# Rebuilding the front of a hybrid MLA and pooling block: scale first, shift as an output row, angles on GpSimd

## The chip, the cores and the metric

The kernel runs on one core of a Trainium2 chip. The metric is the device time of one execution in microseconds (us). Engines are named as the profile names them: PE is TensorE, DVE is VectorE, ACT is ScalarE, POOL is GpSimd, SP is the engine that issues nearly all transfers. "PEld" is PE's weight load.

## The reference, cut to what matters

One encoder block over 1024 tokens of width 1024, in float32. The change touches what comes before attention:

```python
c_act = jax.nn.silu(c)
mod = c_act @ w_ada + b_ada                      # w_ada: 1024 x 6144
sh1, sc1, gt1, sh2, sc2, gt2 = jnp.split(mod, 6)
h = rmsnorm(x, g_mix) * (1.0 + sc1) + sh1
proj = h @ w_in                                  # 960 columns
# proj[..., :448]: q latent 256, kv latent 128, key rope 64; proj[..., 448:]: 4 pool groups of 128
c_q, c_kv = rmsnorm(cq_raw, g_q), rmsnorm(ckv_raw, g_kv)
cos, sin = cos(positions * freqs), sin(positions * freqs)
```

Then come the queries, chunk-causal attention in latent space, the pooling mixer (trailing sums over 2, 4, 8 and 16 tokens, minus u), the output projection gated by gt1, and a SwiGLU network with a last norm.

## The kernel before

Every engine runs a list of instructions written out by hand, in order; semaphores are the only ties between the lists. A float32 matrix product runs as three products of rounded parts (`PASSES`, L46): each operand has a high part (written by `..._hi` functions on POOL or ACT) and a low part, full minus high (the `..._lo` functions and the helper `lo` on DVE, which all show as L1313). x is kept as 8 token tiles of 128; `HT` holds the normed, modulated x transposed, by 8 feature tiles k.

**Modulation.** `w_ada` comes in pieces of 1 MB (`ada_piece`, `load_ada`, L411). DVE sums eight of them, by `accumulate` (L1301, four instructions of 128x512 a piece), to sc1 and gt1 before attention. The 1024 columns of sh1 are done on PE instead (L1868), copied to a row (L892) and turned. The eight sh1 and sc1 pieces come first on SP, then x, then `w_in`.

**Front.** DVE also computes the rope angles (L1322 to L1328, 20 instructions of 128x256 that reduce them by parts of 2 pi), the inverse roots (`inverse_root`, L1266 to L1277, a chain of 12 small instructions) and x times its root (`xn1`, L1309). PE turns a tile of x (`turn_x1`, L1884), ACT scales and shifts it into `HTf` (`modulate1`, L875), POOL takes the high part (`HT`, L673), DVE the low part (`h_lo`). For each token tile PE then runs 24 products against the first 448 columns of w_in (`WTM`, L1900). ACT copies the result to `TMO` and sums its squares (`tm_out`, L883 to L885).

**Between front and attention.** `pool_group(i)` (48 products of 128x512, in the helper `product`, L1841) gives u of a group transposed; `u_out` copies it. `WU` has two slots, so `load_wu(2)` waits for `u_done` 2. DVE norms the latents (`tm_norm`), POOL rotates the keys (L688 to L697, `kr_ready`), rounds `CKV`, `WP` and `WUV` and then runs `windows`: for each of four groups 4, 3, 2 and 1 additions of 128x1024 (L714), two small instructions, and a wait for `pooled(i)` on DVE (L1420). `turn_latents` (L1919) turns `TMO`, with `lt_hi` on ACT and `lt_lo` on DVE behind it. Behind the windows on POOL are eight rotations of the queries (`rotate`, L731 to L735), without which PE's loop of `q_nope`, `q_latent` and `turn_rope` can't run. Attention scores begin at L2015.

## Time and profile before

| | us |
|---|---|
| median of 3 runs | 1037.54 (1037.45 to 1038.49) |
| the profiled execution's own time | 1039.98 |
| its span | 1038.2 |

| engine | busy us | share of span |
|---|---|---|
| PE | 992.2 | 96% |
| PEld | 815.9 | 79% |
| DVE | 676.5 | 65% |
| ACT | 447.7 | 43% |
| POOL | 410.0 | 39% |

The span is the time from the first to the last recorded instruction. Times in rows are from the span's start. A busy PE is a share of time only; PEclk is the clock granted to it, 1.00 being 2.4 GHz and 0.50 being 1.2 GHz. Where PE is busy throughout, what other engines do beside it costs nothing, so the stretches that matter to a change in the front are those in which PE isn't full: the first 46 us and the time from 114 to 182 us.

### The profile page before, as it was taken

Reading aid. Unit: us, or ns where it says so; the run is one execution under the profiler, and the core shown is the slowest. Engines: PE = TensorE matmul, PEld = TensorE weight load, DVE = VectorE, ACT = ScalarE, POOL = GpSimd, SP = SyncE. Lnnn points to the kernel's source line nnn. Section 1 sums busy time; section 2 is a strip of 40 time slices with the busy share of each in tenths; the row PEclk is TensorE's granted clock in tenths of the full one; section 3 lists DMA queues with packets and bytes.
Section 4 is the critical chain, followed back from the end, with each engine's and each line's share of the span. In section 5 each row is a group of like instructions: output and inputs, shape, how many; then the busy total and the mean of one; then the engine's idle time right before and its main releaser. Section 6 shows DMA issues by size and latency. Waiting matters only on the chain.

```text
span 1038.2 us, 12646 instructions
## 1 busy us (share of the span) xinstructions
PE 992.2 (96%) x4605; PEld 815.9 (79%) x4605; DVE 676.5 (65%) x957; ACT 447.7 (43%) x759; POOL 410.0 (39%) x306
## 2 busy tenths in 40 slices
PE   5799989999999999989999999999999999999995
PEld 0598877788888887868888888888888888888884
DVE  5848865767524589956746745844846864747867
ACT  0663246867621466532333333333234442634442
POOL 1313666499603121054643643644642300037510
PEclk9699999999899999989999999999999999999998
DMA  9902110544113333356356255255357998755513
GB/s 325 362 1 102 42 41 1 175 131 127 55 53 111 102 122 101 113 177 207 112 170 205 102 180 186 104 180 182 125 159 261 340 353 312 253 200 172 196 71 153
DMA packets 119929, 165.20 MB, mean 159 GB/s; under 512 B 8694, under 2 KB 61754, under 8 KB 119868
## 3 DMA queue, kind: packets, MB, share of 16 engines
q1 hardware_dynamic: 119868, 164.40, 47.1%
q8 instruction: 37, 0.61, 0.2%
q14 instruction: 24, 0.20, 0.1%
HBM read 124.26 MB, written 40.11 MB: 158 GB/s over the span
## 4 chain that ended last, share of the span: by engine, by line
PE 78%; DVE 11%; ACT 3%; issue 2%; POOL 2%; DMA 2%; SPq 2%; DVEq 0%; POOLq 0%; ACTq 0%
PE PS L2137 39%; PE PS L2171 16%; PE PS L1841 14%; PE PS L1900 4%; PE PS L2015 3%; DMA ADA<-in_w_ada 1%; PE PS L2027 1%; DVE GT L1301 1%; DVE RS L1277 1%; POOL ropeQ L731 1%; ACT PR L986 1%; DVE RT L1273 1%; PE PS L2087 1%; POOL WIN L714 1%; DVE XD L1815 1%
## 5 line engine op out<-in xcount | busy, mean ns | idle before, releaser
L2171 PE MATMUL PS<-RE 128*128 128x512 f32 x924 | 210.5, 390 | 0.0
L2171 PEld LDWEIGHTS PS<-RE 128*128 128x128 f32 x924 | 173.5, 188 | 36.7 <-ACT DU L1217 0.4
L1313 DVE TENSOR_TENSOR RE<-REraw,RE 128x1024 fp32r<-128x1024 f32 x77 | 107.0, 1426 | 73.8 <-ACT RE L1149 73.0
L2137 PE MATMUL PS<-HT,WS 128*128 128x512 f32 x528 | 125.9, 395 | 4.6 <-ACT U L1132 4.6
L1149 ACT ACTIVATE RE<-REraw 128x1024 fp32r<-128x1024 f32 x77 | 81.4, 1061 | 103.3 <-DMA REraw<-t_scratch 67.9
L2137 PE MATMUL PS<-HB,WS 128*128 128x512 f32 x528 | 123.3, 389 | 0.0
L2137 PEld LDWEIGHTS PS<-HT,WS 128*128 128x128 f32 x528 | 100.9, 191 | 26.2 <-issue 5.0
L2137 PEld LDWEIGHTS PS<-HB,WS 128*128 128x128 f32 x528 | 99.2, 188 | 20.5
L2137 PE MATMUL PS<-HT,W 128*128 128x512 f32 x480 | 110.8, 390 | 0.0
L2137 PEld LDWEIGHTS PS<-HT,W 128*128 128x128 f32 x480 | 90.0, 188 | 18.6
L1691 DVE TENSOR_TENSOR SG<-PS,PV 128x512 f32<-128x512 f32 x22 | 15.1, 684 | 106.7 <-PE PS L2137 106.7
L1103 ACT ACTIVATE WS<-WSf 128x1024 fp32r<-128x1024 f32 x42 | 44.6, 1063 | 65.6 <-POOL WSf L791 42.1
L814 POOL TENSOR_TENSOR TW<-TW 128x512 f32<-128x512 f32 x11 | 23.5, 2138 | 111.4 <-PE PS L2137 94.2
L1313 DVE TENSOR_TENSOR WS<-WSf,WS 128x1024 fp32r<-128x1024 f32 x42 | 51.2, 1222 | 20.8 <-POOL WSf L786 14.5
L2137 PE MATMUL PS<-HB,W 128*128 128x512 f32 x264 | 61.6, 389 | 0.0
L783 POOL TENSOR_TENSOR WSf<-W34raw 128x1024 f32<-128x1024 f32 x9 | 21.5, 2391 | 94.9 <-PE PS L2137 94.9
L2137 PEld LDWEIGHTS PS<-HB,W 128*128 128x128 f32 x264 | 49.6, 188 | 10.3
L1142 ACT ACTIVATE SG<-SG 128x512 f32<-128x512 f32 x33 | 20.9, 632 | 78.0 <-DVE SG L1691 78.0
L1841 PE MATMUL PS<-HT,WU 128*128 128x512 f32 x192 | 44.6, 392 | 0.0
L1900 PE MATMUL PS<-WTM,HT 128*128 128x448 f32 x192 | 42.6, 382 | 1.5 <-DVE HT L1313 1.5
L836 POOL TENSOR_TENSOR DP<-DP,GT 128x512 f32<-128x512 f32 x4 | 5.2, 1299 | 98.0 <-DVE GT L1377 98.0
L1841 PEld LDWEIGHTS PS<-HT,WU 128*128 128x128 f32 x192 | 36.0, 188 | 7.8 <-issue 0.5
(261 smaller groups left out, 1874.2 us busy)
## 6 DMA issues: line engine op xcount, KB each, us to landing
REraw<-h_scratch SPq DMA_DIRECT2D x77, 256.0 KB, 4.9
h_scratch<-SG SPq DMA_DIRECT2D x55, 256.0 KB, 2.4
ADA<-in_w_ada SPq DMA_DIRECT2D x12, 1024.0 KB, 8.2
TW<-in_w_down SPq DMA_DIRECT2D x22, 512.0 KB, 4.4
t_scratch<-TW SPq DMA_DIRECT2D x44, 256.0 KB, 5.0
REraw<-t_scratch SPq DMA_DIRECT2D x44, 256.0 KB, 5.1
REraw<-in_w_down SPq DMA_DIRECT2D x33, 256.0 KB, 6.5
X<-in_x SPq DMA_DIRECT2D x16, 512.0 KB, 9.3
```

The lines of the kernel that those rows point to most:

```text
L783: pool.tensor_tensor(WSf[:, SLOT[5], LO], W34raw[:, :, 0:HK], W34raw[:, :, HK:KT], ALU.add).then_inc(S["w_sum"], 1)
L814: then(pool.tensor_tensor(b22, b22, b12, ALU.subtract))
L1103: act.activation(WS[:, SLOT[p], HI], full, ACT.Copy).then_inc(S["w_hi"], 1)
L1142: act.activation(SG[:, q, :], SG[:, q, :], ACT.Silu).then_inc(S["silu"], 1)
L1149: act.activation(RE[e][:, HI], REraw[e][:, LO], ACT.Copy).then_inc(S["d_hi"], 1)
L1313: dve.tensor_tensor(out_, full, hi.bitcast(F32), ALU.subtract).then_inc(ready, 1)
L1691: dve.tensor_tensor(dst, PS[:, y, :], part[:, m, :], ALU.add).then_inc(S["c_add"], 1)
L1841: ins = pe.matmul(ps, l, r, start=(n_ == 0), stop=(n_ == len(terms) - 1))
L1900: ins = pe.matmul(PS[:, 4 + t % 2, 0:TM], HT[:, a, k, tok(t)], WTM[:, b, k, :], start=(k == 0 and p == 0), stop=(k == KT - 1 and p == 2))
L2015: ins = pe.matmul(bank, l, r, start=(z == 0), stop=(z == 4 and not diag))
L2137: ins = pe.matmul(PS[:, bank, :], l, r, start=fresh and z == 0, stop=z == len(terms) - 1, skip_group_check=not fresh)
L2171: ins = pe.matmul(PS[:, D_BASE[p] + j, :], RE[e][:, a, 0, tok(j)], RE[e][:, b, 1, :], start=p in (1, 2, 7) and i == 0 and x_ == 0, stop=i ...
```

## The change

- **Loads.** SP brings the four sc1 pieces (`load_sc1`) in the place of sh1: two at once, then x 0 to 3, half of `WTM`, the other two sc1 pieces, the rest. The sh1 pieces become the first of DVE's list (`DVE_CHUNKS`), later than `sc1_sum` 2. The gt1 pieces get four places of their own (`GTP`), three of which lie where `WTM` is, so pieces 5 to 7 wait for `bias_row` and the latents' `LT` (at 96 KB) waits for `acc_done` 8 on ACT.
- **Scale.** Pieces 0, 1 and 3 are summed on DVE (`scale_sum`), piece 2 on POOL (`ACCP`); PE turns each half (`scale_turn`) and DVE makes four columns of G1 (`scale_columns`), so that the first four feature tiles can go before the scale of the others is known. PE's work on the first four token tiles is split in feature halves.
- **Shift.** ACT only multiplies by G1, straight into the high part of `HT` (`scaled_hi`), and DVE takes the low part from PSUM (`scaled_lo`); `HTf` and POOL's L673 are gone here. sh1 times the 448 columns is one row from 16 narrow products (`shift_row`), spread to all partitions by `shift_all` and added to `TMO` on DVE in four instructions (`tm_bias`). The squares of the latents (`tm_squares`) wait for that and follow `u_out(0)` on ACT.
- **Angles** move from DVE to POOL, each fused instruction as two, ahead of `wtm_hi(0)`. The scaling of x 4 to 7 moves from DVE to POOL.
- **Order behind.** `wu_hi(2)` is ahead of the key rotation on POOL and `wu_lo(2)` ahead of the norms on DVE; the two norms share one `inverse_root`. `accumulate(6)` and `(7)` come between the norms and `CKV`'s low part. `col_sum(2)`, `(3)` and the `gate` copies move from ahead of the last pool group to just ahead of PE's query loop. 40 transposes of the identity (`keep_clock`) stand ahead of the first `scale_turn`.

```diff
...
-    ADA0 = at("ADA0", 32, [P, 4, 4, HALF])
...
-    SHROW = at("SHROW", 180, [P, 2, HALF])
+    ACCP = at("ACCP", 180, [P, HALF])
+    GTP = [at(f"GTP{i}", kb, [P, 4, HALF]) for i, kb in enumerate((0, 96, 104, 112))]
+    BROW = at("BROW", 182, [P, HALF])
...
-    DVE_CHUNKS = (2, 3, 4, 5, 10, 11)
+    DVE_CHUNKS = (0, 1, 4, 5, 10, 11)
...
+        if 4 <= j < 8:
+            return GTP[j - 4][:], sc1_in[j - 4], 32
+        ring, turn = (ADA1, j // 2) if j < 4 else (ADA3, j // 2 - 2)
+        return ring[:, j % 2], ada_in[j % 2], 16 * (turn + 1)
...
+            if j == 0:
+                sp.wait_ge(S["sc1_sum"], 2)
+            elif j in (2, 3, 10, 11):
...
+        load_sc1(0)
+        sp.dma_start(POSI[:], positions.rearrange("b (t p) -> p (b t)", p=P), allow_slow_non_contiguous=True).then_inc(S["pos_in"], 16)
+        sp.dma_start(FREQ[:], freqs.partition_broadcast(P)).then_inc(S["freq_in"], 16)
+        load_sc1(1)
+        load_x(0)
         for src, r, n in ((b_ada, 0, 48), (g_mix, ROW_MIX, 8), (g_ffn, ROW_FFN, 8), (pool_scale, ROW_POOL, 4)):
             sp.dma_start(ROWS[r:r + n, :], src.rearrange("l (r n) -> (l r) n", n=P)).then_inc(S["rows_in"], 16)
-        sp.dma_start(POSI[:], positions.rearrange("b (t p) -> p (b t)", p=P), allow_slow_non_contiguous=True).then_inc(S["pos_in"], 16)
-        sp.dma_start(FREQ[:], freqs.partition_broadcast(P)).then_inc(S["freq_in"], 16)
-        load_sh1(1)
-        load_ada(1)
-        load_sh1(2)
-        load_ada(2)
-        load_sh1(3)
-        load_x(0)
-        load_ada(3)
-        for t in range(1, 4):
-            load_x(t)
-        for i in range(4):
-            sp.dma_start(WTMraw[:, 2 * i:2 * i + 2, :], win_d[:, 2 * i:2 * i + 2, 0:TM]).then_inc(wtm_in[i], 16)
+        load_x(1)
+        load_x(2)
+        load_x(3)
+        load_wtm(0)
+        load_wtm(1)
+        load_sc1(2)
+        load_sc1(3)
+        load_wtm(2)
+        load_wtm(3)
...
-        sp.wait_ge(S["sh1_rows"], 1)
+        sp.wait_ge(S["sc1_sum"], 1)
         load_wu(0)
         load_wu(1)
+        for j in range(3):
+            load_ada(j)
+        sp.wait_ge(S["t1"], 2 * KT)
+        sp.dma_start(WPraw[:], w_pool.rearrange("l g c d -> c (l g) d")).then_inc(S["wp_in"], 16)
         load_ada(4)
+        load_ada(3)
+        sp.wait_ge(S["acc_done"], 4)
+        sp.dma_start(WUQraw[:], wuq_d).then_inc(S["wuq_in"], 16)
+        sp.dma_start(WUKraw[:], w_uk.rearrange("l c h d -> c (l h) d")).then_inc(S["wuk_in"], 16)
+        sp.wait_ge(S["bias_row"], B["bias_row"] + 1)
+        sp.dma_start(WUVraw[:], w_uv.rearrange("l c h v -> c (l h) v")).then_inc(S["wuv_in"], 16)
         load_ada(5)
-        sp.wait_ge(S["t1"], NT)
-        sp.dma_start(WPraw[:], w_pool.rearrange("l g c d -> c (l g) d")).then_inc(S["wp_in"], 16)
         load_ada(6)
         load_ada(7)
-        sp.wait_ge(S["tm_done"], NT)
-        sp.dma_start(WUVraw[:], w_uv.rearrange("l c h v -> c (l h) v")).then_inc(S["wuv_in"], 16)
         sp.wait_ge(S["u_done"], 2)
         load_wu(2)
         sp.wait_ge(S["u_done"], 4)
         load_wu(3)
-        sp.wait_ge(S["acc_done"], 8)
...
+        pool.wait_ge(S["cast"], B["cast"] + 1)
+        pool.wait_ge(S["freq_in"], 16)
+        for t in range(NT):
+            ins = pool.tensor_scalar(ANG[:, t, :], FREQ[:], POSF[:, t:t + 1], 0.0, ALU.mult, ALU.add)
+        then(ins)
+        for turns in (4096.0, 1.0):
+            then(pool.tensor_scalar(TURN[:], ANG[:], float(1 / (2 * np.pi * turns)), ROUND_MAGIC, ALU.mult, ALU.add))
+            then(pool.tensor_scalar(TURN[:], TURN[:], -ROUND_MAGIC, 0.0, ALU.add, ALU.add))
+            for part in two_pi_parts():
+                then(pool.tensor_scalar(SHALF[:], TURN[:], -part * turns, 0.0, ALU.mult, ALU.add))
+                ins = pool.tensor_tensor(ANG[:], SHALF[:], ANG[:], ALU.add)
+                if (turns, part) != (1.0, two_pi_parts()[-1]):
+                    then(ins)
+        ins.then_inc(S["ang_ready"], 1)
...
+        wtm_hi(0)
+        wtm_hi(1)
+        pool.wait_ge(S["act_silu"], 1)
+        pool.wait_ge(sc1_in[2], 16)
+        then(pool.tensor_scalar(ACCP[:], ADAS[:, 2, 0, :], CS[:, 0:1], 0.0, ALU.mult, ALU.add))
+        for t in range(1, 4):
+            then(pool.tensor_scalar(ADAS[:, 2, t, :], ADAS[:, 2, t, :], CS[:, t:t + 1], 0.0, ALU.mult, ALU.add))
+            ins = pool.tensor_tensor(ACCP[:], ACCP[:], ADAS[:, 2, t, :], ALU.add)
+            if t < 3:
+                then(ins)
+        ins.then_inc(S["sc1_part"], 1)
+        wtm_hi(2)
+        wtm_hi(3)
+        pool.wait_ge(S["rs1"], 2)
+        for t in range(4, NT):
+            pool.tensor_scalar(X[:, t, :], X[:, t, :], RS[:, t:t + 1], 0.0, ALU.mult, ALU.add).then_inc(S["xn1"], 1)
...
+        wu_hi(2)
+        pool.wait_ge(S["tm_bias"], B["tm_bias"] + 4)
         pool.wait_ge(S["trig_ready"], 1)
         pool.memset(U[:, :, 0:PADW], 0.0)
         keys = TMO[:, :, QR + LAT:TM].rearrange("p t (a d) -> p t a d", a=2)
         then(pool.tensor_tensor(both[:, :, :, 1], twice(ropeK[:, 1, :, 0]), twice(ropeK[:, 0, :, 1]), ALU.add))
         pool.memset(WIN[:, :, 0:PADW], 0.0).then_inc(S["kr_ready"], 1)
-        wu_hi(2)
...
+        def scaled_hi(q):
+            hf, k = divmod(q, KT)
+            act.wait_ge(S["t1"], q + 1)
+            act.wait_ge(S["modcols"], 1 if k < 4 else 2)
+            act.activation(HT[:, HI, k, half(hf)], PS[:, k % 4, :], ACT.Copy, scale=G1[:, k:k + 1]).then_inc(S["h_hi"], 1)
...
+            act.activation(TMO[:, t, 0:TM], PS[:, 4 + t % 4, 0:TM], ACT.Copy).then_inc(S["tm_out"], 1)
+        def tm_squares(t):
+            act.wait_ge(S["tm_bias"], B["tm_bias"] + t // 2 + 1)
+            act.activation(JUNK2[:, 0:QR], TMO[:, t, 0:QR], ACT.Square, accum_out=SS[:, t:t + 1])
+            act.activation(JUNK2[:, QR:QR + LAT], TMO[:, t, QR:QR + LAT], ACT.Square,
+                           accum_out=SS[:, 8 + t:9 + t]).then_inc(S["tm_sq"], 1)
+            act.wait_ge(S["tm_sq"], B["tm_sq"] + t + 1)
...
+        for t in range(4):
             squares1(t)
-        for t in range(NT):
-            modulate1(t)
-            if t < 4:
-                squares1(t + 4)
-            if t >= 3:
-                tm_out(t - 3)
-        for t in range(NT - 3, NT):
+        for q in range(4):
+            scaled_hi(q)
+        for t in range(4, NT):
+            squares1(t)
+        for q in range(4, KT):
+            scaled_hi(q)
+        tm_out(0)
+        tm_out(1)
+        for q in range(KT, KT + 4):
+            scaled_hi(q)
+        tm_out(2)
+        tm_out(3)
+        for q in range(KT + 4, 2 * KT):
+            scaled_hi(q)
+        act.wait_ge(S["ang_ready"], 1)
+        act.activation(SHALF[:], ANG[:], ACT.Sin, scale=0.5)
+        act.activation(SQUART[:], ANG[:], ACT.Sin, scale=0.25).then_inc(S["sin_ready"], 1)
+        for t in range(4, NT):
             tm_out(t)
+        act.wait_ge(S["bias_row"], B["bias_row"] + 1)
+        act.activation(BROW[0:2, 0:TM], PS[0:2, 3, 0:TM], ACT.Copy).then_inc(S["bias_out"], 1)
...
         u_out(0)
+        for t in range(NT):
+            tm_squares(t)
         u_out(1)
+        act.wait_ge(S["acc_done"], 8)
         for t in range(4):
             lt_hi(t)
...
+        dve.tensor_copy(POSF[:], POSI[:]).then_inc(S["cast"], 1)
...
+        def scaled_lo(q):
+            hf, k = divmod(q, KT)
+            dve.wait_ge(S["h_hi"], q + 1)
+            dve.scalar_tensor_tensor(HT[:, LO, k, half(hf)], PS[:, k % 4, :], G1[:, k:k + 1],
+                                     HT[:, HI, k, half(hf)].bitcast(F32), ALU.mult, ALU.subtract).then_inc(S["h_ready"], 1)
...
+        scale_sum(ACC[:, 0], 0, 1)
+        dve.wait_ge(S["rowsT"], 1)
+        dve.tensor_copy(COLS[:], PS[:, 6, 0:N_ROWS]).then_inc(S["cols"], 1)
+        dve.wait_ge(S["cols"], 1)
+        scale_columns(0)
+        roots1(0, 4)
+        scaled_lo(0)
+        wtm_lo(0)
+        scaled_lo(1)
+        scaled_lo(2)
+        wtm_lo(1)
+        scaled_lo(3)
+        scale_sum(ACC[:, 1], 3)
+        roots1(4, 4)
+        scale_columns(1)
+        scaled_lo(4)
+        wtm_lo(2)
+        scaled_lo(5)
+        wtm_lo(3)
+        scaled_lo(6)
+        scaled_lo(7)
+        accumulate(0)
+        for q in range(KT, KT + 4):
+            scaled_lo(q)
...
+        for q in range(KT + 4, 2 * KT):
+            scaled_lo(q)
...
+        accumulate(1)
+        accumulate(2)
         wu_lo(1)
+        accumulate(3)
+        dve.wait_ge(S["colsum"], 2)
+        then(dve.tensor_tensor(MOD[:, 0:8], PS[:, 2, 0:8], COLS[:, 0:8], ALU.add))
+        pair = SHP[:].rearrange("p (k a) -> p k a", a=2)
+        then(dve.tensor_copy(pair[:, :, HI], MOD[:, 0:8]))
+        lo(pair[:, :, LO], MOD[:, 0:8], pair[:, :, HI], S["sh1_ready"])
...
+        dve.wait_ge(S["bias_all"], B["bias_all"] + 1)
+        shift = PS[:, 2, 0:TM].rearrange("p (o n) -> p o n", o=1).broadcast_to([P, 2, TM])
+        for i in range(4):
+            dve.tensor_tensor(TMO[:, 2 * i:2 * i + 2, 0:TM], TMO[:, 2 * i:2 * i + 2, 0:TM], shift, ALU.add).then_inc(S["tm_bias"], 1)
+        accumulate(5)
+        wu_lo(2)
+        dve.wait_ge(S["tm_sq"], B["tm_sq"] + NT)
+        dve.tensor_scalar(VAR[:, 0:8], SS[:, 0:8], 1.0 / QR, EPS, ALU.mult, ALU.add)
+        then(dve.tensor_scalar(VAR[:, 8:16], SS[:, 8:16], 1.0 / LAT, EPS, ALU.mult, ALU.add))
+        inverse_root(None, None, 16, None, S["rs1"])
+        dve.wait_ge(S["rs1"], 3)
...
+        accumulate(6)
+        accumulate(7)
...
-        accumulate(6)
...
-        accumulate(7)
...
+        def scale_turn(i):
+            pe.wait_ge(S["sc1_acc"], i + 1)
+            if i == 1:
+                pe.wait_ge(S["sc1_part"], 1)
+            for k in range(4):
+                col = PS[:, 7, 8 + 4 * i + k:9 + 4 * i + k]
+                ins = pe.matmul(col, ACC[:, i, k * P:(k + 1) * P], ONES[:, 0:1], start=True, stop=i == 0)
+                if i == 1:
+                    ins = pe.matmul(col, ACCP[:, k * P:(k + 1) * P], ONES[:, 0:1], start=False, stop=True)
+            ins.then_inc(S["sc1_sum"], 1)
...
+        keep_clock(40)
+        scale_turn(0)
+        turn_x1(0, 0, range(4))
+        project(0, 0, 4)
+        project(1, 0, 4)
+        project(2, 0, 4)
+        scale_turn(1)
+        turn_x1(0, 4, range(4))
+        project(3, 0, 4)
+        project(0, 4, KT)
+        project(1, 4, KT)
+        turn_x1(1, 0, range(4, NT))
+        project(2, 4, KT)
+        project(3, 4, KT)
+        turn_x1(1, 4, range(4, NT))
+        for t in range(4, NT):
+            project(t, 0, KT)
+            if t == 5:
+                col_sum(0)
+            if t == 6:
+                col_sum(1)
...
+                    ins = pe.matmul(PS[0:2, 3, 0:TM], SHP[:, 2 * k:2 * k + 2], WTM[:, a, k, :],
...
+        shift_row()
+        pool_group(0, (0,))
+        shift_all()
+        pool_group(0, (1,))
         pool_group(1)
+        pool_group(2, (0,))
...
+        pool_group(2, (1,))
         for t in range(4, NT):
             turn_latents(t)
-        col_sum(2)
-        col_sum(3)
         pool_group(3)
...
+        pe.wait_ge(S["wuk_ready"], 1)
+        col_sum(2)
+        col_sum(3)
...
```

## Rows read from the trace of the kernel before

**Rows 1.** Chain that ended last, 46 to 183 us: start us, us, what.
```profile
46.40 7.34 PE PS L1900 x24
...
65.22 0.87 PE PS L1884 x8
66.10 4.85 PE PS L1900 x24
...
92.14 21.78 PE PS L1841 x96
...
131.96 1.91 POOL WIN L714
...
153.47 2.42 POOL ropeQ L731 x2
...
182.16 2.32 PE PS L2015 x10
```

**Rows 2.** Windows of stretches: us, busy us (instructions) by engine, PEclk, DMA, GB/s.
```profile
52.00:92.00 40.00, 40.00 (x218) 37.20 (x217) 22.00 (x39) 23.25 (x77) 8.38 (x7) 1.00 0.05 12
```

**Rows 3.** Timeline, first landings: start us, us, engine, line, operation.
```profile
9.53 0.49 DVE L1299 TENSOR_SCALAR ACC<-ADA,CS 128x512 f32<-128x512 f32 x1 [9.53 <-DMA ADA<-in_w_ada]
```

**Rows 4.** Groups of instructions by line and form: busy us, mean ns.
```profile
L1328 DVE SCALAR_TENSOR_TENSOR ANG<-TURN,ANG 128x256 f32<-128x256 f32 x10 | 4.3, 425 | 0.3
...
L1313 DVE TENSOR_TENSOR QN<-PS,QN 128x512 fp32r<-128x512 f32 x8 | 5.5, 692 | 11.2 <-ACT QN L970 11.1
```

**Rows 5.** Groups by line and form, POOL, 0 to 300 us: busy us, mean ns.
```profile
L731 POOL TENSOR_TENSOR ropeQ<-QRAW,COS 128x256 f32<-128x256 f32 x8 | 5.9, 739 | 5.4 <-DVE U L1420 3.3 <-PE PS L1982 1.6
...
L705 POOL TENSOR_SCALAR WP<-WPraw 128x512 fp32r<-128x512 f32 x1 | 0.6, 619 | 0.0
```

**Rows 6.** Timeline of POOL, the first window sums, 118 to 125 us.
```profile
118.12 1.38 POOL L677 TENSOR_SCALAR WU<-WUraw 128x1024 fp32r<-128x1024 f32 x1
119.47 5.11 POOL L714 TENSOR_TENSOR WIN<-WIN 128x1024 f32<-128x1024 f32 x2
```

**Rows 7.** Chain, `accumulate(6)` beside those sums, one step of `accumulate(7)` alone.
```profile
120.07 2.28 DVE GT L1301
...
122.37 2.77 DVE GT L1301
...
128.29 0.76 DVE GT L1301
```

**Rows 8.** Timeline, 95 to 102 us: small DVE instructions beside POOL and alone.
```profile
95.32 1.43 POOL L688 TENSOR_TENSOR ropeK<-TMO,COS 128x256 f32<-128x256 f32 x2
...
96.11 0.65 DVE L1275 TENSOR_TENSOR RT<-RS 128x8 f32<-128x8 f32 x1
...
98.19 0.17 DVE L1275 TENSOR_TENSOR RT<-RS 128x8 f32<-128x8 f32 x1
...
101.44 3.26 DVE L1397 SCALAR_TENSOR_TENSOR TMO<-TMO,RS,GQ 128x256 f32<-128x256 f32 x8
```

**Rows 9.** Timeline of the front: transposes, x's scaling, the squares of a latent.
```profile
36.77 3.67 PE L1884 MATMUL PS<-IDENT,X 128*128 128x128 f32 x16 [2.56 <-DVE X L1309]
...
53.46 1.42 DVE L1309 TENSOR_SCALAR X<-X,RS 128x1024 f32<-128x1024 f32 x2
...
59.11 0.38 ACT L884 ACTIVATE JUNK<-PS 128x256 f32<-128x256 f32 x1
```

**Rows 10.** Timeline, the third pool group's weights: issue, then their rounding.
```profile
103.05 0.37 SPq L447 DMA_DIRECT2D WUraw<-in_w_in  x1
...
106.98 1.07 POOL L677 TENSOR_SCALAR WU<-WUraw 128x1024 fp32r<-128x1024 f32 x1 [6.03 <-DMA WUraw<-in_w_in]
```

**Rows 11.** Timeline, 110 to 132 us: normed latents reach POOL, first window copy, column sum.
```profile
110.11 1.97 POOL L701 TENSOR_SCALAR CKV<-TMO 128x1024 fp32r<-128x1024 f32 x1 [2.06 <-DVE TMO L1402]
...
130.65 1.22 DVE L1420 SCALAR_TENSOR_TENSOR U<-WIN,U 128x1024 f32<-128x1024 f32 x1
130.67 1.13 PE L1853 MATMUL PS<-GT,ONES 128*128 128x512 f32 x2 [1.52 <-DVE GT L1301]
```

239 lines of the change are left out of this document (98 added, 141 removed).

## The prediction

> **What bounds the kernel now.** The page comes first: PE is busy for 96% of the span, so a change in the front can pay only where PE waits or does other work than before. The chain that ended last gives these places [rows 1]. PE's products of the front begin at 46.40 us; from there it runs without a gap, shown for 52 to 92 us in [rows 2]: a tile of x is eight transposes of 0.87 and 24 products of 4.85 together. The pool groups begin at 92.14 (I call this point S). From 114 on the chain leaves PE: window sums on POOL (131.96) and query rotations on POOL (153.47) lead to the first scores at 182.16. Behind that all work is released by other work, so what is won or lost at 182 us is won or lost at the end. Three places are to be priced: the start to S, S to the rotations (61.3 us), the rotations to the scores (28.7 us).
>
> **What POOL and DVE do to each other.** This decides the case. One step of an accumulation takes 0.76 us on DVE alone, and 2.28 and 2.77 beside POOL's window sums [rows 7]; the two sums that fall there take 5.11 where one is 1.9 [rows 1, 6]. 1.9 + 1.9 + 0.76 is 4.6: they take turns, and each waits for the other's whole instruction. Small ones do too: 0.65 instead of 0.17 beside a rotation of 0.74, and one gets through at 98.19, where POOL itself had to wait for a semaphore [rows 8]. I price it so: a DVE instruction that reads SBUF starts when POOL's current one ends (some 0.2 us early) and puts POOL off by 0.55; those that read PSUM keep their 0.69 [rows 4] and are free of it.
>
> **Part 1, start to S.** Removed: the sh1 row on PE, its copy, 20 angle instructions of DVE (0.43 each [rows 4]), POOL's roundings of x.
> - Landings: before, 2.1 MB are there at 9.53 [rows 3]. Now 1 MB of sc1 is ahead of the positions: taken at 7 us; the second piece again at 9.5.
> - Angles on POOL: an addition of 128x256 is 0.74, a 128x512 multiplication 0.62 [rows 5]; for 128x256 I take 0.40 (an estimate between that and half of it). 8 small ones at 0.2, 14 at 0.40, 10 at 0.74 and 24 gaps of 0.08 (the semaphore steps) make 16.5. DVE's eight steps for the scale and four scalings of x put them off by about 7. POOL is through at 31.6 (7.2 + 16.5 + 7, rounded up by the order), `wtm_hi(0)` at 32.6, `wtm_lo(0)` one turn later at 34.4.
> - The other way to the first product: scale summed at 15; 40 transposes in front of `scale_turn(0)`, from 12 us (their list waits for `ROWS`, behind 2.6 MB), 0.23 each at first, as in [rows 9], later half of that, as in [rows 1], to 19; G1 at 21; the roots at 25 (two small steps per POOL instruction); x scaled at 29.4 (0.71 [rows 9] and a turn each); `scaled_lo(0)` at 31.5. So the wait for POOL ends last, and the first product is at 34.5 instead of 46.4.
> - Then DVE and POOL have to do, by turns, the rest of WTM (six of 1.0), POOL's part of the scale (4 of 0.62, 3 of 1.3), piece 3 on DVE (4 of 0.76), roots (2.3), four scalings of x; the low part of the first four features ends at 38.5, the scale's second half is ready at 44.2, G1's at 47.6, `scaled_lo(7)` at 53.3. PE has 36 products of 0.20 and 4 us of small ones and transposes up to there, and waits for some 5 us.
> - From 53.9 PE is full again: 12 + 24 products and the second half's turns 10.8, four tiles of 4.85, two column sums 2.1 (like the one of 1.13 [rows 11]), shift row 16 x 0.19 = 3.1. S is at 89.4, 2.7 earlier. Of 12 us won at the first product 9 are lost again. The sh1 pieces lie in this: `accumulate(3)` ends at 79, `col_sum(1)` needs it at 80; a late piece would cost one for one.
>
> **Part 2, S to the rotations.** PE: half a pool group 5.45, `shift_all` 1.1, the rest to S+12.0 and S+22.9, `pool_group(2)`'s half to S+28.4. Beside it:
> - shift added on DVE, four of 1.1, to S+11; `accumulate(5)` to S+14. Then `wu_lo(2)`: its weights are only asked for after `u_done` 2 (S+12.0), and issue to rounding takes 3.9 and 1.1 [rows 10]: S+17.1. On SP, gt1's pieces 5 to 7 and `WUV` are ahead of those weights, 3.4 MB at S, but at the rate of [rows 3] and better they are in by S+12. Queued behind that wait are the norms on DVE and, on POOL, the key rotation. `tm_squares` ends at S+19.3 (eight times 0.38 and three shorter [rows 9]). 13 steps of the root beside the key rotation end at S+24.7, 16 norm products (3.26 for the first eight [rows 8]) at S+30.2. Before, POOL gets the normed latents at 110.11 [rows 11], S+18.0: 12.2 later. PE waits 1.8 for its first transposes.
> - `accumulate(6)` and `(7)` now stand between the norms and everything of the latents, and ACT waits for `acc_done` 8. They fall beside CKV, WP, WUV, the window sums and `wu_hi(3)` on POOL, eight instructions of 11 us in all, and eight steps of DVE by turns: 11 + 8 x 0.55 is S+45.8. Then CKV's low part, four `lt_lo`, `wu_lo(3)` S+51.3, `pooled(0)` S+52.7; before it started at 130.65 [rows 11], S+38.5. PE has no work from S+38 to S+48.
> - From `pooled(0)` on it is the chain of before (windows 1 to 3, about 22.8 from its start to 153.47), less 1.2 for the gate copies that move away. Rotations at S+74.3 instead of S+61.3: 13.0 later.
>
> **Part 3, rotations to scores.** `col_sum(2)` and `(3)` are now ahead of `q_nope(0)`: 2 x 1.13 [rows 11] in a loop in which PE and POOL await one another; bounds 0 and 2.3, I take 1.9, since q_nope has nothing else in front of it. Their old place is worth nothing: PE waits there for `accumulate(7)` as it is.
>
> **Sum.** -2.7 + 13.0 + 1.9 = +12.2. On the profiled execution's 1039.98 that is 1052.2, on the median of 1037.54, which lies 2.4 lower, 1049.7.
>
> **A rule of the Trainium skill.** For a fused addition of DVE the rows have 0.43 and for POOL's 0.74, a ratio of 1.7 [rows 4, 5]. The Trainium skill (GPSIMD Engine Reference, section 3.1) measures 1.96 for an addition of 2048 elements; by it the ten additions would be 0.9 longer in all (an estimate from that page). By its section 8, GpSimd contends with DVE instructions that have two SBUF inputs or run in a 2-port mode, without a price; the trace agrees, and gives the price.
>
> **Rivals.**
> 1. *Faster: the two engines hinder each other less than I charge.* It decides at two places: whether POOL has the angles done by 24 us instead of 31.6, and whether `accumulate(6)`, `(7)` run at 0.76 a step. Then S is 8 earlier (the first product near 27, PE warm and full sooner), tm_norm is at S+27, lt_lo(0) at S+35, PE's pool groups go through, and the rotations start at S+60: -8 - 1.5 + 1.9 = -7.6, 1030. For it: plain chains of small steps leave gaps, and some of POOL's recorded time is not port time. Against: [rows 6 to 8]. Chance 0.17.
> 2. *Front as in rival 1, middle as forecast*: -8 + 13 + 1.9 = +7, 1044.5. For it: the angle instructions are short. Chance 0.13.
> 3. *Slower still: in the front only one small DVE step gets through per POOL instruction.* The roots then end at 28.5 and x at 33, products begin at 36.5, every turn of the next part is a full instruction, and S is 3.5 later than before; in the middle the same adds 2.4: +3.5 + 15.4 + 1.9 = +20.8, 1058.3. For it: the 0.65 beside back-to-back instructions [rows 8]. Against: these chains wait for semaphores. Chance 0.18.
> 4. *No change*: a shorter stall behind acc_done 8 meets the gain of the front, within 0.2% (2.1 us, what a measurement of this kernel can tell). Chance 0.06.
>
> **Chances and range.** The forecast has 0.46, its own range 1046 to 1055. Slower by over 0.2%: 0.46 + 0.13 + 0.18 = 0.77; same 0.06; faster 0.17. The range goes from 1034, which takes in rivals 2 and 4 and leaves out most of rival 1, to 1059, which takes in rival 3.
>
> **What would show it.** In the profile of the changed kernel: (1) the last angle addition on POOL near 31 us and the first front product near 34.5, released by DVE's low part of WTM; (2) DVE's scale steps above 1 us each; (3) S near 89; (4) the root chain behind `wu_lo(2)`, waiting for POOL's WU; (5) the steps of `accumulate(6)`, `(7)` at 1.5 to 2.7 and ACT's first `LT` copy released by DVE's GT; (6) a hole of some 10 us in PE before the second four transposes of the latents; (7) first rotation near 164, first scores near 194. I am wrong if `accumulate(6)` to `(7)` take 6 us, or if the weights of the third group land so early that the norms don't wait.

## The result and the profile after

The changed kernel takes 1052.13 us (median of four runs, 1049.83 to 1054.30) against 1037.51 (four runs of the kernel before beside them): a ratio of 1.014, 95% interval 1.0124 to 1.0156: slower by 1.4%. Its profiled execution took 1052.04 us with a span of 1050.0; that of before took 1039.98 with 1038.2.

The chain that ended last in the changed kernel (start us, us, what) shows the three stretches of the prediction:

```profile
53.55 3.97 PE PS L1980 x18
...
90.56 5.46 PE PS L1923 x24
...
163.21 2.41 POOL ropeQ L774 x2
...
193.32 2.32 PE PS L2140 x10
```

The first product (shown below) stands at 34.30 instead of 46.40, the pool groups at 90.56 instead of 92.14, the first rotation at 163.21 instead of 153.47, the first scores at 193.32 instead of 182.16 [rows 1]. The front gives back 10.5 of the 12.1 us that it won, and the stretch behind it loses 11.3. From the scores to the end of the span it is 856.7 us against 856.0, so between these two executions nearly all of the difference lies ahead of the scores.

The front, from the timeline of POOL (start us, us, engine, line, operation; in brackets the idle time before it and what ended that):

```profile
8.94 4.18 POOL L684 TENSOR_SCALAR ANG<-FREQ,POSF 128x32 f32<-128x32 f32 x8 [4.85 <-DMA FREQ<-freqs]
...
30.68 0.72 POOL L691 TENSOR_TENSOR ANG<-SHALF,ANG 128x256 f32<-128x256 f32 x1
31.38 1.83 POOL L698 TENSOR_SCALAR WTM<-WTMraw 128x896 fp32r<-128x896 f32 x2
```

of DVE:

```profile
23.80 3.93 DVE L1362 TENSOR_SCALAR X<-X,RS 128x1024 f32<-128x1024 f32 x4
29.07 0.75 DVE L1384 SCALAR_TENSOR_TENSOR HT<-PS,G,HT 128x512 fp32r<-128x512 f32 x1 [1.34 <-ACT HT L914]
32.34 1.81 DVE L1366 TENSOR_TENSOR WTM<-WTMraw,WTM 128x896 fp32r<-128x896 f32 x1 [2.52 <-POOL WTM L698]
```

and of PE:

```profile
34.30 10.38 PE L1980 MATMUL PS<-WTM,HT 128*128 128x448 f32 x36 [5.40 <-DVE WTM L1366]
44.52 0.28 PE L1951 MATMUL PS<-ONES,ACC 128*128 128x1 f32 x2
```

The angles begin at 8.94, when their frequencies have landed, and end at 31.4. WTM's first rounding waits behind them, DVE's half of it (32.34) behind that, and the first product behind that; the feature of x that it needs too had been ready at 29.8. The 36 products that follow take 10.38 us. PE had stood idle for 4.39 and 5.40 us before them, and its granted clock is 0.50 from 25 to 40 us. Up to 40.2 us a product starts every 0.37 us, from there on every 0.21; the mean of all is 0.29. The groups of PE from 35 to 40 us and from 41 to 44 us (busy us, mean ns of one; the records of neighbours overlap):

```profile
L1980 PE MATMUL PS<-WTM,HT 128*128 128x448 f32 x15 | 6.0, 590 | 5.4 <-DVE WTM L1366 5.4
...
L1980 PE MATMUL PS<-WTM,HT 128*128 128x448 f32 x16 | 3.5, 368 | 0.0
```

The middle, DVE:

```profile
97.07 4.08 DVE L1472 TENSOR_TENSOR TMO<-TMO,PS 128x896 f32<-128x896 f32 x4 [9.10 <-PE PS L2021]
...
120.67 12.57 DVE L1354 SCALAR_TENSOR_TENSOR GT<-GTP,CS,GT 128x512 f32<-128x512 f32 x8
133.28 3.25 DVE L1366 TENSOR_TENSOR CKV<-TMO,CKV 128x1024 fp32r<-128x1024 f32 x1
...
141.44 1.21 DVE L1504 SCALAR_TENSOR_TENSOR U<-WIN,U 128x1024 f32<-128x1024 f32 x1
```

and, in the same stretch, ACT's first copy of a turned latent and PE's second group of turns:

```profile
133.28 0.49 ACT L963 ACTIVATE LT<-PS 128x384 fp32r<-128x384 f32 x1 [19.13 <-DVE GT L1354]
```

```profile
137.34 3.01 PE L2038 MATMUL PS<-IDENT,TMO 128*128 128x128 f32 x13 [9.09 <-DVE KRT L1366]
```

The eight steps of `accumulate(6)` and `(7)` take 12.57 us, where alone they would take 6.1 (0.76 each [rows 7]). ACT had waited 19.13 us for them, and PE stands idle for 9.09.

The kernels of the experiments below stand in the same table. Their distances are given from the start of the pool groups, S, so that a front that came out a little sooner doesn't hide in them. "Rotation to scores" is in us:

| kernel | S | norms done | pooled(0) | first rotation | rotation to scores | scores at |
|---|---|---|---|---|---|---|
| before | 92.14 | S+17.9 | S+38.5 | S+61.3 | 28.7 | 182.16 |
| forecast | 89.4 | S+30.2 | S+52.7 | S+74.3 | 30.6 | 194.3 |
| changed | 90.56 | S+30.2 | S+50.9 | S+72.7 | 30.1 | 193.32 |
| angles late | 90.45 | S+30.2 | S+50.9 | S+72.7 | 32.1 | 195.29 |
| sums cut | 88.79 | S+30.3 | S+45.0 | S+66.9 | 30.2 | 185.87 |
| squares first | 88.51 | S+26.0 | S+47.9 | S+69.7 | 31.2 | 189.41 |
| column sums back | 90.59 | S+30.2 | S+50.9 | S+72.6 | 28.7 | 191.92 |
| pieces early | 88.44 | S+30.3 | S+45.0 | S+66.8 | 30.2 | 185.40 |
| middle reordered | 88.79 | S+36.5 | S+36.4 | S+66.4 | 30.2 | 185.40 |
| angles late, idle transposes | 89.5 | S+30.7 | S+51.3 | S+73.1 | 31.4 | 193.98 |
| idle transposes | 88.81 | S+30.2 | S+50.9 | S+72.7 | 30.1 | 191.64 |
| all of these | 88.53 | S+36.5 | S+36.4 | S+68.5 | 28.7 | 185.80 |
| window 0 early | 89.13 | S+37.2 | S+37.1 | S+66.9 | 30.1 | 186.17 |
| the same, angles late | 90.55 | S+37.2 | S+37.1 | S+66.5 | 30.2 | 187.18 |
| window 0 behind roots | 91.27 | S+34.2 | S+34.1 | S+64.4 | 30.2 | 185.80 |

### The profile page after: what moved, and what is told of

Read it like the earlier page. It is cut to its first block, busy times and chain, and to the rows that moved or that the text cites. A ratio compares the mean times of both kernels' runs of the same rounds, so it can differ in the third digit from the quotient of the medians.

```text
span 1050.0 us, 12710 instructions
## 1 busy us (share of the span) xinstructions
PE 987.8 (94%) x4639; PEld 819.7 (78%) x4639; DVE 682.6 (65%) x925; ACT 436.2 (42%) x711; POOL 436.1 (42%) x341
## 4 chain that ended last, share of the span: by engine, by line
PE 77%; DVE 11%; POOL 5%; ACT 3%; issue 2%; DMA 1%; SPq 0%; POOLq 0%; DVEq 0%; ACTq 0%
PE PS L2262 39%; PE PS L2296 16%; PE PS L1923 12%; PE PS L1980 4%; PE PS L2140 3%; POOL WIN L757 1%; DVE GT L1354 1%; DVE RS L1330 1%; PE PS L2152 1%; POOL ANG L691 1%; ACT PR L1038 1%; POOL ropeQ L774 1%; DMA FREQ<-freqs 1%; PE PS L2212 1%; DVE RT L1326 1%
## 5 line engine op out<-in xcount | busy, mean ns | idle before, releaser
L2296 PEld LDWEIGHTS PS<-RE 128*128 128x128 f32 x924 | 173.5, 188 | 36.4 <-issue 0.5
L2262 PEld LDWEIGHTS PS<-HT,W 128*128 128x128 f32 x480 | 90.9, 190 | 18.9
L1980 PEld LDWEIGHTS PS<-WTM,HT 128*128 128x128 f32 x192 | 37.4, 200 | 11.7 <-issue 6.9
```

Source lines behind the costliest of these rows:

```text
L1980: ins = pe.matmul(PS[:, 4 + t % 4, 0:TM], HT[:, a, k, tok(t)], WTM[:, b, k, :], start=(k == 0 and p == 0), stop=(k == KT - 1 and p == 2), ...
L2262: ins = pe.matmul(PS[:, bank, :], l, r, start=fresh and z == 0, stop=z == len(terms) - 1, skip_group_check=not fresh)
L2296: ins = pe.matmul(PS[:, D_BASE[p] + j, :], RE[e][:, a, 0, tok(j)], RE[e][:, b, 1, :], start=p in (1, 2, 7) and i == 0 and x_ == 0, stop=i ...
```

## The experiments

The kernels of each comparison ran between runs of the kernel before on the same chip, whose medians were 1038.27, 1037.12, 1037.27 and 1037.13 us in the order told here (angles late, sums cut, squares first and column sums back; pieces early, middle reordered, idle transposes and all of these; window 0 early and the two others with angles late; the last). All differences of single kernels below some 2 us are read from the traces.

### The angles late

The angle block of POOL is moved as a whole:

```diff
-        pool.wait_ge(S["cast"], B["cast"] + 1)
...
-        ins.then_inc(S["ang_ready"], 1)
         wtm_hi(0)
         wtm_hi(1)
...
         wu_hi(0)
         wu_hi(1)
+        pool.wait_ge(S["cast"], B["cast"] + 1)
...
+        ins.then_inc(S["ang_ready"], 1)
         wu_hi(2)
```

> The changed kernel with one move: the angle instructions on POOL stand behind the rounding of the first two pool groups' weights instead of ahead of the first piece of WTM. Theory (POOL and DVE take turns, and POOL's angle chain sets the first product): without POOL's chain beside it DVE's scale and root steps run at 0.76 and 0.20, the first front product is at about 29 us instead of 34.3, PE is full from 47 instead of 53.6, the pool groups begin near 84 instead of 90.6, and the rest keeps its distances: 6.5 us faster than the changed kernel, about 1045.5. Rival (the tail of the front waits for the sh1 pieces, whose loads and sums come late): the second column sum waits for accumulate(3), the pool groups don't begin before 88, at most 2.5 us faster.

Measured: 1053.83 us (1053.23 to 1055.03), ratio 1.0152 [1.0134, 1.0169], and S at 90.45. Nothing is gained. That lies within the rival's "at most 2.5 us faster", but not for its reason: PE goes from its products into the second column sum (81.17) without a wait, and the pool groups follow as before. The timeline of DVE and PE in the front:

```profile
25.65 5.97 DVE L1362 TENSOR_SCALAR X<-X,RS 128x1024 f32<-128x1024 f32 x4
32.96 0.75 DVE L1384 SCALAR_TENSOR_TENSOR HT<-PS,G,HT 128x512 fp32r<-128x512 f32 x1 [1.34 <-ACT HT L914]
33.62 1.08 DVE L1366 TENSOR_TENSOR WTM<-WTMraw,WTM 128x896 fp32r<-128x896 f32 x1
```

```profile
34.85 10.50 PE L1980 MATMUL PS<-WTM,HT 128*128 128x448 f32 x36 [2.06 <-DVE WTM L1366]
```

POOL is free of the angles, and the first product is no earlier: 34.85. What gets in the way now is POOL's next work. Its share of the scale starts at 21.98, when its piece lands, and runs beside DVE's roots and scalings of x: the scalings start at 25.65 instead of 23.80 and take 5.97 us for the four instead of 3.93, the first feature is begun at 32.96 instead of 29.07, and WTM's low part, which DVE takes behind it, at 33.62. In the changed kernel the short angle steps (0.4 and 0.7) were what stood beside DVE there, and they cost it less than the 1.3 us additions do. What the wait for the angles cost, 4.5 us from the feature to the product, is lost again to the same contention in another place.

### Idle transposes, and both together

The second experiment on the front gives PE something to do in its idle time, so that the clock is up when the products come:

```diff
         keep_clock(40)
         scale_turn(0)
+        keep_clock(28)
         turn_x1(0, 0, range(4))
+        keep_clock(36)
         project(0, 0, 4)
```

> The changed kernel with 28 more idle transposes on PE behind the first column sums of the scale and 36 more behind the first turn of x, in stretches in which PE otherwise waits for DVE. Nothing else differs. In the changed kernel the granted clock is 0.50 from 25 to 40 us, the first 36 products take 10.4 us (0.29 each) and end when the second column sums start, at 44.5. Theory (PE's clock, not the scale's sum, sets the second column sums): granted clock near 1.0 from 25 us on, first product still at 34 to 34.5, the 36 products in 7.8 to 8.2 us, second column sums at 42, pool groups at 88 to 88.5 instead of 90.6, median 1049 to 1050. Rival (the scale's second half, summed on DVE and POOL, is ready at 44 and sets the end): products end at 42, second column sums still at 44 to 44.5, pool groups at 90 to 90.6, median within 0.5 us of the changed kernel's.

Measured: 1049.86 us (1048.01 to 1051.31), ratio 1.0126 [1.0104, 1.0149], S at 88.81. PE:

```profile
34.69 7.58 PE L1980 MATMUL PS<-WTM,HT 128*128 128x448 f32 x36
42.44 0.35 PE L1951 MATMUL PS<-ONES,ACC 128*128 128x1 f32 x2 [0.18 <-POOL ACCP L708]
```

0.21 us a product instead of 0.29 in the mean, as the theory has it, and the second column sums begin at 42.44 instead of 44.52. The wait in front of them, 0.18, is for POOL's share of the scale: the rival's bound is there, but at 42.4 and not at 44. The first product is later than it might be, since my own 36 transposes run until 34.6.

The gain of 1.8 us in S isn't theirs, though. In "middle reordered", whose front is that of the changed kernel without them, S is at 88.79 too:

```profile
33.50 9.87 PE L1980 MATMUL PS<-WTM,HT 128*128 128x448 f32 x36 [3.56 <-DVE WTM L1366]
43.21 0.28 PE L1951 MATMUL PS<-ONES,ACC 128*128 128x1 f32 x2
...
51.74 4.03 PE L1980 MATMUL PS<-WTM,HT 128*128 128x448 f32 x18 [1.05 <-DVE HT L1384]
```

0.8 us won at the column sums are gone again where PE gets full, 51.81 against 51.74, since there PE waits for DVE's features in both. What S goes with is the end of the first eight angle steps. They end between 11.5 and 12.4 us in all seven kernels with the angles in their place that have S at 88.4 to 89.1, and at 13.1 and 13.2 in the changed kernel and in "column sums back", with S at 90.6. This isn't the landing of the frequencies alone: in "window 0 early" the eight steps begin last of all, at 10.08, and end at 12.37, and in the changed kernel they begin at 8.94 and take 4.18 us. Beside the one microsecond there stands one at the first product (33.3 to 33.6 against 34.3, without idle transposes) and two at S. The clock may have its part in that, with 0.50 from 35 to 40 us in the changed kernel and 0.70 to 0.85 in "pieces early", "squares first" and "sums cut". The last kernel is outside this rule: its angle steps end at 11.9, and S is at 91.27, with a granted clock of 0.91 from 50 to 70 us, where the others have 1.00. No edit moves these eight steps alone, so that they set S is read from the order of the kernels and not shown.

With the angles late as well, and fewer transposes:

```diff
         scale_turn(0)
+        keep_clock(24)
         turn_x1(0, 0, range(4))
+        keep_clock(12)
```

> The changed kernel with the angles behind the second WU on POOL, as in the first experiment, and with 24 and 12 idle transposes on PE as in the one with idle transposes. All the work is done. Theory (the first experiment missed because the angles' end and DVE's scaling of x stood within 0.6 us of each other as bounds of the first product, and because PE's clock and the scale's second half bound what follows): first product no earlier than 34, 36 products in 7.6 us instead of 10.5, pool groups at 88 to 88.6, no better than with the idle transposes alone. Rival (POOL's angles hold the front up, and the low clock hid what taking them away gives): first product at 32 or earlier, pool groups at 86 or earlier.

Measured: 1049.36 us (1047.02 to 1049.75), ratio 1.0104 [1.0084, 1.0125], first product at 34.73, S at 89.5. Here the products stop once more, for WTM's second half:

```profile
34.73 1.46 PE L1980 MATMUL PS<-WTM,HT 128*128 128x448 f32 x6
37.00 6.43 PE L1980 MATMUL PS<-WTM,HT 128*128 128x448 f32 x30 [0.81 <-DVE WTM L1366]
43.27 0.28 PE L1951 MATMUL PS<-ONES,ACC 128*128 128x1 f32 x2
```

Taking the angles away gives the front nothing here either, as the theory said, though S is 1 us later than it had it. So at the first product the angles and POOL's share of the scale lead to the same time within half a microsecond, at the second column sums PE's clock and POOL's share of the scale within two, and behind them the features' pace takes over. Neither of the two edits, nor both, wins much there.

### The sums cut

`accumulate(6)` and `accumulate(7)` add one column each instead of 4 x 512.

```diff
-            for t in range(4):
+            for t in range(1 if j in (6, 7) else 4):
                 cs = CS[:, 4 * kh + t:4 * kh + t + 1]
+                if j in (6, 7):
+                    ins = dve.scalar_tensor_tensor(acc[:, 0:1], buf[:, t, 0:1], cs, acc[:, 0:1], ALU.mult, ALU.add)
```

> The changed kernel with accumulate(6) and accumulate(7) cut to one column each (the sum of gt1's second half is left out, so the time lacks 12.6 us of DVE). Theory (these two sums, by turns with POOL's window sums, hold back all of the latents): PE's hole before the second four latent transposes closes, the first window copy starts 8 to 9 us earlier, and so do the rotations: 8.5 us faster, about 1043.5. Rival (the window sums on POOL, which start when the norms end, set the time, and the sums on DVE only stretch them): only the 4.4 us of turns are won, about 1047.7. A second rival (the late norm is all of it): no change within 1 us.

Measured: 1047.45 us (1044.95 to 1048.42), ratio 1.0092 [1.0072, 1.0112]. Rotations at S+66.9 instead of S+72.7: 5.7 us, between the rival's 4.4 and the theory's 8.5. The chain says where the rest stays:

```profile
129.25 3.25 POOL WIN L757
...
133.77 1.24 DVE U L1506
```

The two sums' 12.6 us are gone from DVE, but POOL's window sums of group 0, which only begin when the norms are done, are the next chain, and with them `pooled(0)` comes 5.9 us earlier, not 12.6.

### The squares first

ACT squares the latents ahead of its second copy of U. The third WU's rounding goes behind the key rotation on POOL, and its low part behind the norms on DVE.

```diff
-        u_out(0)
+        u_out(0, (0,))
         for t in range(NT):
             tm_squares(t)
+        u_out(0, (1,))
...
         accumulate(5)
-        wu_lo(2)
         dve.wait_ge(S["tm_sq"], B["tm_sq"] + NT)
...
+        wu_lo(2)
         accumulate(6)
```

> The changed kernel with the latents' squares on ACT ahead of the second half of u_out(0), and the third group's weights rounded behind the key rotation (POOL) and behind the norms (DVE) as before. Theory (the norms are late because ACT waits for the second half group before it squares, and DVE for the weights before it makes roots): squares end 5 us earlier, the norms 5 to 6 us, accumulate(7) and the rotations about 5: about 1047. Rival (the norms can't be used earlier, since PE's half group and the window sums behind it end when they did): 0 to 1 us.

Measured: 1050.10 us (1045.52 to 1051.81), ratio 1.0107 [1.0077, 1.0137]. The norms are done at S+26.0 instead of S+30.2, `pooled(0)` is 3.0 earlier and the rotations 3.0. DVE:

```profile
109.16 3.25 DVE L1483 SCALAR_TENSOR_TENSOR TMO<-TMO,RS,GQ 128x256 f32<-128x256 f32 x8
...
114.43 1.21 DVE L1367 TENSOR_TENSOR WU<-WUraw,WU 128x1024 fp32r<-128x1024 f32 x1
115.57 14.69 DVE L1355 SCALAR_TENSOR_TENSOR GT<-GTP,CS,GT 128x512 f32<-128x512 f32 x8
130.29 1.22 DVE L1367 TENSOR_TENSOR CKV<-TMO,CKV 128x1024 fp32r<-128x1024 f32 x1
...
136.42 1.22 DVE L1505 SCALAR_TENSOR_TENSOR U<-WIN,U 128x1024 f32<-128x1024 f32 x1
```

So 4.2 us won at the norms shrink to 3.0. The missing 1.2 is the third WU's low part (1.21), which the edit itself puts between the norms and the sums. The two sums take 14.69 us instead of 12.57, but CKV's low part behind them takes 1.22 instead of 3.25: from the start of the sums to its end it is 15.9 us in both kernels. POOL's last window addition falls on the last step of the sums here and on CKV's low part there, and costs the same.

### The column sums back

```diff
+        col_sum(2)
+        col_sum(3)
         pool_group(3)
...
         pe.wait_ge(S["wuk_ready"], 1)
-        col_sum(2)
-        col_sum(3)
         for i in range(NT):
             q_nope(i)
```

(with the two gate copies of DVE back in front of WUQ).

> The changed kernel with the two column sums of gt1 and their copies where they stood before (ahead of the last pool group on PE, behind the latents' low parts on DVE). Theory (in their new place they delay PE's query loop by 1.4 us, in the old one they are hidden in the wait behind accumulate(7)): 1 to 1.9 us faster, about 1050.7. Rival (the loop waits for POOL's rotations, so the column sums are hidden there too): no change.

Measured: 1047.50 us (1045.97 to 1052.45), ratio 1.0097 [1.0067, 1.0127]; the profiled execution took 1052.45, S is at 90.59 and the scores at 191.92. The runs scatter by more than the effect, so it is read from the trace:

```profile
163.23 2.42 POOL ropeQ L774 x2
...
191.92 2.30 PE PS L2140 x10
```

From rotation to scores it is 28.7 us, to the tenth what the kernel before has, against 30.1. The two column sums cost 1.4 where they now stand; the middle is untouched by their return (S+72.6).

### The pieces early

The pieces 5 to 7 go into the buffers of the first four, so that DVE can sum 5 and 6 while it waits for the bias row, and 7 right behind the bias; ACT's wait for `acc_done` 8 falls away. On SP the loads of WUQ and WUK go behind the pieces.

```diff
+        accumulate(5)
+        accumulate(6)
         dve.wait_ge(S["tm_out"], NT)
         dve.wait_ge(S["bias_all"], B["bias_all"] + 1)
...
-        accumulate(5)
+        accumulate(7)
         wu_lo(2)
...
-        accumulate(6)
-        accumulate(7)
         dve.wait_ge(S["ckv_hi"], 1)
...
-        act.wait_ge(S["acc_done"], 8)
```

> The changed kernel with pieces 5, 6 and 7 of the first gate loaded into the buffers of pieces 0 to 3, as soon as these come free. DVE sums pieces 5 and 6 in its 9.1 us of idle time before the bias row has arrived, and piece 7 right after the bias adds, so that nothing of accumulate(6) and (7) stands behind the norms; ACT no longer waits for the eighth piece before it copies the latents. The loads of WUQ and WUK go behind the pieces. All the work is still done. Theory (DVE's order in the middle sets the path; the accumulates behind the norms cost the rotations what cutting them cost, 5.7 us counted from the pool groups' start): pooled(0) 45 us behind the pool groups' start instead of 51, first rotation 67 instead of 72.7, scores 5 to 6 us earlier, median about 1046.5. Rival (work moved into the stretch before the pool groups only moves the cost: the pieces' loads push WU's, or DVE's sums meet POOL's copies there): the pool groups start 2 to 5 us later than at 90.6 and the median stays at 1050 to 1053.

Measured: 1044.97 us (1042.96 to 1047.11), ratio 1.0076 [1.0057, 1.0095]. The milestones are those of "sums cut" to a tenth (S+45.0, S+66.8), with all the work done: the theory's numbers. The scores stand at 185.40. What the two sums cost, they cost by their place: ahead of the norms the same work costs nothing at these milestones.

### The middle reordered, and all edits together

Besides the pieces early: ACT's squares first, and on POOL the third WU behind the key rotation and group 0's windows ahead of the fourth WU and of the latents. The windows don't come ahead of the third WU, as the expectation says; POOL rounds it at 106.87 and begins them at 110.04. DVE still takes its low part ahead of the roots.

```diff
+        wu_hi(2)
-        pool.wait_ge(S["tm_norm"], NT)
-        pool.tensor_scalar(CKV[:, HI], TMO[:, :, QR:QR + LAT], 1.0, 0.0, ALU.mult, ALU.add).then_inc(S["ckv_hi"], 1)
...
+            if i == 0:
+                wu_hi(3)
+                pool.wait_ge(S["tm_norm"], NT)
+                pool.tensor_scalar(CKV[:, HI], TMO[:, :, QR:QR + LAT], 1.0, 0.0, ALU.mult, ALU.add).then_inc(S["ckv_hi"], 1)
             pool.wait_ge(S["pooled"], i + 1)
...
+        pooled(0)
         lt_lo(0)
```

> The kernel before this one in the list (pieces early), and besides: ACT's squares of the latents stand ahead of its copy of the first half of U's second part, and POOL builds the windows of group 0 before it copies the third and fourth WU and the latents. All the work is done. Theory (the middle is a chain of DVE's and POOL's order and nothing else holds it): norms 20.7 us behind the pool groups' start instead of 24.8, pooled(0) at about 32 instead of 51, first rotation at about 58 to 62 instead of 72.7, median 1038 to 1042. Rival (the rotations then wait for the latents' turn and the products of WUQ on PE, which depend on the norms alone, or DVE's own sum of work is the bound): first rotation no earlier than 67, as with the pieces alone, median about 1046.

Measured: 1043.46 us (1041.40 to 1045.71), ratio 1.0059 [1.0041, 1.0077]. `pooled(0)` is at S+36.4 and the first rotation at S+66.4, no better than with the pieces alone: the rival's number. But its reason is only half of it. The norms are not earlier but 6 us later, S+36.5. DVE and PE:

```profile
116.20 2.23 DVE RT L1329
```

```profile
119.29 3.92 DVE L1485 SCALAR_TENSOR_TENSOR TMO<-TMO,RS,GQ 128x256 f32<-128x256 f32 x8
```

```profile
125.36 3.68 PE L2038 MATMUL PS<-IDENT,TMO 128*128 128x128 f32 x16 [8.19 <-DVE TMO L1487]
```

```profile
130.00:150.00 20.00, 20.00 (x105) 17.00 (x105) 13.67 (x17) 6.56 (x16) 12.30 (x9) 0.98 0.00 1
```

One step of the root, 128 x 16, takes 2.23 us beside a window sum of POOL, three others 1.75 to 1.77; the roots take 9.7 us where they took 5.6 with the pieces alone. PE, which waited 2 us for the norms there, waits 8.19, and then it is busy without a gap (20.00 of 20.00 us). What windows gained, roots lost. The roots met the windows because they begin late: the third WU's low part stands in front of them on DVE and waits for POOL's rounding, so they begin at 109.51 (S+20.7), where "squares first", with that low part behind the norms, begins them at S+14.7.

All edits together (this one, the column sums back, the idle transposes):

> All edits together: pieces early, squares early, group 0's windows first, the column sums 2 and 3 with their gates back in their old place, and the idle transposes. All the work is done. Theory (the costs stand one behind the other and add up): gains of the middle (10 to 14 us), of the column sums (1.4) and of the clock (0 to 2) add, scores at 176 to 181 us instead of 193.3, median 1034 to 1040, so about level with the kernel before or a little faster. Rival (they share a bound: with the middle short, the column sums or WUQ's products wait for DVE): scores no earlier than 186, median 1044 or more.

Measured: 1043.45 us (1042.06 to 1044.40), ratio 1.0058 [1.0041, 1.0075], scores at 185.80: the rival. The column sums, 1.4 us dear behind the rotations, now cost 2.1 ahead of them (S+68.5 against S+66.4), where PE had no idle time left in "middle reordered". From S to the scores it is 97.3 against 96.6: an edit that was worth 1.4 alone costs 0.7 in this company.

### Group 0's windows early, with and without the angles late

POOL stood idle for 6.6 us between the rope keys and the end of the norms. On top of the pieces early the windows go there, CKV, WP, WUV and the fourth WU behind them. PE gets 24 and 24 idle transposes in the front (24 and 12 with the angles late):

```diff
+            if i == 0:
+                pool.wait_ge(S["tm_norm"], NT)
+                pool.tensor_scalar(CKV[:, HI], TMO[:, :, QR:QR + LAT], 1.0, 0.0, ALU.mult, ALU.add).then_inc(S["ckv_hi"], 1)
...
+                wu_hi(3)
             pool.wait_ge(S["pooled"], i + 1)
...
+        pooled(0)
+        dve.wait_ge(S["ckv_hi"], 1)
```

> The kernel with pieces 5 to 7 early, and besides: POOL builds group 0's windows right behind the rope keys, where it was idle for 6.6 us until the norms were done, and copies the latents, WP, WUV and the fourth WU behind them; DVE takes pooled(0) right behind the norms. 24 idle transposes on PE stand behind the first column sums of the scale and 24 behind the first turn of x. All the work is done. Theory (with the pieces early, POOL's windows are the chain; filling its idle time takes them off, and large POOL adds beside the norms cost DVE only about 0.7 us, while beside the roots they cost 5 as in the kernel with all of the middle reordered): norms begin 25 us behind the pool groups' start, pooled(0) at 31 instead of 45, first rotation at 57 to 61 instead of 66.8, scores at 176 to 181 us, median 1035 to 1040, level with the kernel before. Rival (PE's own work from the pool groups on is the bound, as in the kernel with all of the middle reordered, where it was busy without a gap from 129 to 150 us and the first rotation still stood at 66.4): first rotation at 65 or later, median 1043 to 1045.

Measured: 1042.53 us (1041.73 to 1043.82), ratio 1.0044 [1.0027, 1.0062]. Rotation at S+66.9: the rival's number again, and again by the norms, which end at S+37.2:

```profile
112.98 1.78 DVE L1328 SCALAR_TENSOR_TENSOR RT<-RT,VAR 128x16 f32<-128x16 f32 x1
...
115.00 1.76 DVE L1327 TENSOR_TENSOR RT<-RS 128x16 f32<-128x16 f32 x1
...
118.79 5.40 DVE L1484 SCALAR_TENSOR_TENSOR TMO<-TMO,RS,GQ 128x256 f32<-128x256 f32 x8
```

```profile
112.83 1.89 POOL L751 TENSOR_TENSOR WIN<-U 128x1024 f32<-128x1024 f32 x1
114.81 6.33 POOL L751 TENSOR_TENSOR WIN<-WIN 128x1024 f32<-128x1024 f32 x3
```

```profile
126.35 3.68 PE L2039 MATMUL PS<-IDENT,TMO 128*128 128x128 f32 x16 [8.83 <-DVE TMO L1486]
```

The root's steps of 128 x 16 take 0.17 and 1.76 to 1.78 in turn, beside POOL additions of 1.9: for each POOL addition DVE gets two small steps done, one that is held up and one that isn't.

> The first kernel of this call with the angles behind the second WU on POOL as well, and 12 idle transposes behind the first turn of x instead of 24. All the work is done. Theory: the same within 1 us as the first kernel of this call, since the angles set nothing that another chain doesn't set within 0.6 us. Rival: 2 us faster than it or more, with the pool groups at 86 or earlier.

Measured: 1042.93 us (1039.12 to 1046.55, ten runs), ratio 1.0055 [1.0038, 1.0072]: the same as without, as the theory had it. The first product is 2 us later here (36.32), S at 90.55.

### Group 0's windows behind the roots

The squares first again; POOL waits for the end of the roots before it builds the windows, and the third WU's low part goes between roots and norms. It also has the pieces early, the windows' order of the kernels before it, and 24 and 16 idle transposes.

```diff
         pool.memset(WIN[:, :, 0:PADW], 0.0).then_inc(S["kr_ready"], 1)
+        wu_hi(2)
+        pool.wait_ge(S["rs1"], 3)
...
         dve.wait_ge(S["rs1"], 3)
+        wu_lo(2)
```

> The kernel with pieces 5 to 7 early and group 0's windows behind the rope keys, in which the windows met DVE's roots and made three of their small steps 1.76 us each (norms done 37 us behind the pool groups' start, PE idle for 8.8 us). Here ACT's squares come first, POOL copies the third WU behind the rope keys and then waits for the end of the roots before it builds the windows, and DVE takes the third WU's second half between roots and norms. 24 and 16 idle transposes. All the work is done. Theory (what POOL's large adds meet decides: beside small dependent steps each costs DVE up to 1.8 us, beside the 16 longer norms 2 us in all; PE needs 29 us from the norms' end to the first rotation, as in the last kernel): norms done at 29 to 31, PE's hole 0 to 2 us, pooled(0) at 30 to 32, first rotation at 58 to 61 instead of 66.8, scores at 177 to 180 us if the pool groups start at 88.5, median 1033 to 1037, level with the kernel before or up to 4 us faster. Rival (another order of the same work only moves the meeting again): norms done at 34 or later or first rotation at 65 or later, median 1040 to 1043.

Measured: 1038.12 us (1037.13 to 1040.98, twelve runs) against 1037.13 (seventeen runs), ratio 1.0007 [0.9997, 1.0016]: level with the kernel before. The norms are done at S+34.2, the rival's side, and the first rotation stands at S+64.4, between the two. DVE and POOL:

```profile
111.71 0.17 DVE L1331 SCALAR_TENSOR_TENSOR RS<-RT,RS 128x16 f32<-128x16 f32 x1
...
113.06 10.25 DVE L1486 SCALAR_TENSOR_TENSOR TMO<-TMO,RS,GQ 128x256 f32<-128x256 f32 x8
```

```profile
111.97 2.93 POOL L752 TENSOR_TENSOR WIN<-U 128x1024 f32<-128x1024 f32 x1 [1.57 <-DVE RS L1331]
114.97 6.47 POOL L752 TENSOR_TENSOR WIN<-WIN 128x1024 f32<-128x1024 f32 x3
```

Eight of the roots' eleven steps are back at 0.17 (the other three stand beside the key rotation), but the first eight norms, with all four additions of POOL beside them, take 10.25 us instead of 3.26. I had charged them 2 us more, from "window 0 early", where only the last of POOL's four additions fell on them. Still, this order is 8.3 us better from S to the scores than the changed kernel (94.5 against 102.8).

Two things are left in this kernel that its order doesn't show. From the norms to the first rotation the chain runs over PE, and PE had waited for the norms; its granted clock is 0.50 from 124.6 to 131.4 us. The same sixteen transposes, from the chain, right behind the wait and 10 us later:

```profile
125.47 3.68 PE PS L2041 x16
...
135.73 1.75 PE PS L2041 x16
```

The 24 products between them take 6.58, where the 48 behind them take 10.94, 5.47 for 24. So some 3 us of the way to the first rotation are the low clock (an estimate from these rows). The transposes behind the norms take the same 3.68 in "middle reordered" and "window 0 early".

"Level" doesn't mean that the scores are level, either. They stand at 185.80 against 182.16, 3.6 us later, and from there to the end of the span it is 853.2 us against 856.0. PE is at the lower level for 18.9 us of that stretch, in the kernel before for 23.1. The stretch takes 853.1 to 854.5 us in the six kernels with more than the 40 idle transposes of the changed kernel, and 855.6 to 858.5 in the eight others, the kernel before and the changed one among them. These are single executions, and that the idle transposes are the cause is not shown. Between the two profiled ones (1040.98 and 1039.98 us) the near-level time is 3.6 us lost ahead of the scores and 2.8 won behind them.

## Why the prediction was right

The time came out at 1052.1 where 1049.7 was forecast, inside the range and on the side that had 0.77. The mechanism is the forecast one: the front wins little, and what is lost between the pool groups and the rotations is more. The sizes of single steps were off by 0.5 to 3 us, in part against one another. Step by step:

- **First product, 34.5 forecast, 34.30 measured.** The angles end at 31.4 (31.6, though its terms, 7.2 + 16.5 + 7, add up to 30.7), WTM's low part starts at 32.34 and ends at 34.1 (34.4), and the wait for POOL ends last, as put. The other way was ready at 29.8, earlier than the 31.5 of the forecast: the roots ended at 23.8 (25) and the scalings of x at 27.7 (29.4); they took 3.93 for four, where 2.8 would be alone [rows 9], so the turns charge 0.5 us too much beside POOL's short steps. That it was the wait for the angles which cost the front was my theory afterwards, and "angles late" refutes it: without them POOL's share of the scale does the same. The 36 products behind the first were put at 0.20 us each, 7.2 in all, and took 10.38, since the first of them ran at the lower clock; the forecast had that at nothing. It cost little, since PE waited for features behind them as it was.
- **S, 89.4 forecast, 90.56 measured: -1.6 instead of -2.7.** PE is full from 53.55 (53.9), so the miss is behind that. It has 18 + 24 products and 32 turns to do for 12.3 us up to 65.88, where I counted 36 products and 10.8, and two of the four tiles take 5.06 instead of 4.85. The shift row took 3.27 (3.1), a column sum 0.78 (1.05). Other kernels with the same front have S at 88.4 to 88.8 (or 90.6), so single executions spread by 2 us in this term.
- **Norms at S+30.2, forecast S+30.2.** `wu_lo(2)` ends at S+18.9 (17.1), the squares end at S+19.2 (19.3), the roots at S+24.8 (24.7). "Squares first", which takes both out from in front of the roots, shows that they were the wait: the norms are 4.2 earlier. Which of the two counts for how much it doesn't tell; they end within 0.4 us of each other.
- **The two sums, end at S+45.8 forecast, S+42.7 measured.** 12.57 us where I had 15.6 (by its terms, 11 + 8 x 0.55, it is 15.4). The turns are there, but not in each step: the chain has 0.67, 1.43, 0.99, 0.99 and then 2.27, 2.27, 1.42, 2.27. The shorter ones stand beside POOL's copies (CKV's 1.49, WP's and WUV's 1.04 and 1.05, WU's 1.36), the long ones beside window sums. Of the 3.1 us that were charged too much, 1.3 are lost again before `pooled(0)`: CKV's low part takes 3.25 beside those sums, and 1.62 in "pieces early". `pooled(0)` at S+50.9 (52.7), rotations +11.3 instead of +13.0. The hole in PE was 9.1 us, where "some 10" stood. "Sums cut" and "pieces early" show that the place of these sums was dear: they take 5.7 and 5.9 us off the way from S to the rotations.
- **Column sums, +1.9 forecast, +1.4 measured**, shown by their return.
- **The sum at the scores: -1.6 + 11.3 + 1.4 = +11.2 (12.2).** With 0.7 us more behind the scores this is the 11.8 by which the two spans differ; the profiled execution came out at 1052.04, where the sum against the profiled time of before gave 1052.2. This closeness is in part luck, since the front missed by 1.1 us one way and the middle by 1.7 the other. The medians differ by more, 14.6. The forecast put 12.2 on the median of before and came out 2.4 too low, and this is the step that was mis-sized: it took the distance between two single executions for the distance between two medians. What executions of one kernel differ by goes with the clock. Of the 50 runs of the kernel before beside the experiments, the 11 with a mean granted clock of 0.980 or less took 1038.27 to 1040.17 us, the 15 with 0.984 or more 1034.84 to 1037.71. The profiled execution of before, at 0.980, is a long one for its kernel; that of after, at 0.978, lies in the middle of its own, whose four have 0.976 to 0.981. Whether the change itself lowers the clock is not shown.
- **Rivals.** That the engines hinder each other less (1) is refuted where it counts: the angles end at 31.4 and not at 24, and the sums take 12.6 and not 6. The slower steps in the front (3) are refuted too: the roots were done at 23.8 us, not at 28.5. A faster front with this middle (2) and a stall that just meets the gain (4) would have needed S some 6 us earlier or a middle 10 us shorter.

What stays open: why the clock falls in one kernel and not in another whose code is the same there. "Angles late", "squares first" and "angles late, idle transposes" have a granted clock of 0.85, 0.91 and 0.91 from 150 to 170 us where the changed kernel has 1.00, and their way from rotation to scores is 2.0, 1.1 and 1.3 us longer; their edits end long before. The windows of that stretch in the changed kernel and in "angles late" (us, busy us by engine, clock, DMA, GB/s):

```profile
150.00:170.00 20.00, 15.55 (x89) 12.55 (x88) 13.98 (x13) 11.77 (x22) 16.11 (x16) 1.00 0.00 1
```

```profile
150.00:170.00 20.00, 14.74 (x77) 12.00 (x76) 13.92 (x13) 11.04 (x20) 16.16 (x16) 0.85 0.00 1
```

## What to carry to other kernels

Before a chain is moved onto a free engine, ask what will run beside it: here an idle POOL was cheap only where DVE read PSUM or waited, and dear beside small dependent DVE steps or 16 short norms. Ask of every moved wait what stands behind it on its queue; the same two sums cost nothing ahead of the norms, where DVE had idle time, and 5.7 us behind them. And work that is taken from one place lets the next work of its queue move up: when an experiment that removes a wait gains nothing, look first at what now runs in its place. A sum of distances from two traces forecasts one execution; for a median, take into the range what executions of one kernel differ by (here 5 us).

## What the runs showed of the hardware

- Large additions on POOL (128 x 1024, 1.9 us alone) beside DVE: a DVE step of 128 x 16 goes from 0.17 to 1.76 us and, once, 2.23; a step of 128 x 512 from 0.76 to between 2.27 and 2.77; eight norms of 128 x 256 from 3.26 to 5.40 and 10.25, by how many of POOL's additions fall on them. POOL's own additions go from 1.89 to between 1.92 and 2.40 beside root steps and norms, and up to 3.29 elsewhere. DVE's subtractions with one operand in PSUM keep their 0.54 and 0.28 beside the same additions.
- Beside back-to-back window additions of POOL, two small steps of DVE's root chain get done per addition: one of 1.76, one of 0.17 ("window 0 early", "middle reordered").
- PE at the lower of its two levels (granted clock 0.50) starts a product of 128x448 every 0.37 us, at the upper one every 0.20 to 0.21; a transpose every 0.21 instead of 0.11 [rows 1]. With 64 idle transposes in its idle time the granted clock was 0.89 from 25 to 40 us, where it was 0.50.
- The first angle step, which waits for the small load of the frequencies, starts between 7.85 and 10.08 us in kernels whose queues are the same up to there, and the eight steps then take 2.3 to 4.2 us.
- Among 50 runs of the kernel before, those with a mean granted clock of 0.980 or less took 1038.3 to 1040.2 us, those with 0.984 or more 1034.8 to 1037.7.
